# Stationary weight blocks 64 bytes further on, and products before a norm that end tile by tile

## What is computed

```
# first block, two layers i; (h: 256 tokens, hc: 256 context tokens)
h = h + 0.5 * m2 * (silu(a) * b) @ ffn_w_out[i, 0]      # a, b = split(modnorm(h) @ ffn_w_in[i, 0])
y = fourier(modnorm(h)) @ fnet_w_out                    # i = 0
y = (silu(g) * norm(retention(q, k, v))) @ ret_w_out    # i = 1; q, k, v, g = modnorm(h) @ ret_w_in
h = h + m5 * y
h = h + 0.5 * m8 * (silu(a) * b) @ ffn_w_out[i, 1]
...
# second block, two layers l
f = (silu(n @ ff1_w_gate) * (n @ ff1_w_up)) @ ff1_w_down     # n = rmsnorm(h, pre)
h = h + 0.5 * rmsnorm(f, post)
m = concat(ssd, pool, attention)(rmsnorm(h) @ w_in) @ w_out
h = h + rmsnorm(m, mix_post)
f = (silu(n @ ff2_w_gate) * (n @ ff2_w_up)) @ ff2_w_down
h = h + 0.5 * rmsnorm(f, post)
```

## Time and profile before

| | us |
|---|---|
| median of 3 runs | 2917.98 |
| lowest and highest | 2908.57, 2922.2 |
| profiled execution | 2915.53 |
| its span, first to last instruction | 2913.7 |
| TensorE busy in it | 2789.5 |
| VectorE busy | 1703.9 |
| ScalarE busy | 1153.1 |
| mean granted TensorE clock | 0.987 of full speed |

### The profile page before, as it was taken

One profiled execution on the slowest core, in us unless ns is written; L12 is line 12 of the kernel. 1 busy time (PEld: TensorE's weight loads), 2 busy tenths in 40 slices (PEclk: granted clock), 3 DMA queues, 4 the chain that ended last, 5 costly groups with the idle time before them and its releaser, 6 DMA issues.

```text
span 2913.7 us, 43918 instructions
## 1 busy us (share of the span) xinstructions
PE 2789.5 (96%) x18214; PEld 2496.8 (86%) x18214; DVE 1703.9 (58%) x2029; ACT 1153.1 (40%) x1442; POOL 0.9 (0%) x13
## 2 busy tenths in 40 slices
PE   6999999999999999999999999999989999998998
PEld 3878878778887888878998999999779999997897
DVE  3774654677325753443356655655766566576764
ACT  4322224422224223243254544444545444454443
POOL 0000000000000000000000000000000000000000
PEclk8999999999999999999999999999999999999999
DMA  6654531456233663634223565664326656642463
GB/s 234 195 177 132 172 121 37 130 181 187 92 98 102 202 188 106 195 101 125 88 87 123 173 187 166 178 212 130 119 75 200 192 156 194 188 124 68 149 184 120
DMA packets 371094, 428.69 MB, mean 147 GB/s; under 512 B 13952, under 2 KB 351104, under 8 KB 370816
## 3 DMA queue, kind: packets, MB, share of 16 engines
q1 hardware_dynamic: 370224, 424.79, 47.6%
q10 hardware_dynamic: 720, 1.74, 0.2%
HBM read 425.43 MB, written 1.05 MB: 146 GB/s over the span
## 4 chain that ended last, share of the span: by engine, by line
PE 85%; DVE 8%; ACT 4%; issue 2%; DMA 1%; SPq 0%; DVEq 0%; ACTq 0%
PE ps L949 25%; PE ps L950 25%; PE ps L951 25%; PE ps L967 3%; ACT w_hi L678 1%; DVE w_lo L687 1%; PE ps L1106 1%; DVE rstd L1096 1%; DMA raw<-in_w_mod 1%; PE ps L1275 1%; DVE tmp L1201 1%; PE ps L773 1%; DVE cx L1778 1%; DVE h L1206 1%; PE ps L1653 0%
## 5 line engine op out<-in xcount | busy, mean ns | idle before, releaser
L687 DVE TENSOR_TENSOR w_lo<-raw,w_hi 128x1024 fp32r<-128x1024 f32 (+1 forms) x672 | 800.0, 1199 | 898.5 <-ACT w_hi L678 891.9
L949 PE MATMUL ps<-u_hi,w_hi 128*128 128x256 f32 (+1 forms) x3520 | 1123.1, 319 | 37.8 <-DVE w_lo L687 8.9
L951 PE MATMUL ps<-u_hi,w_lo 128*128 128x256 f32 (+1 forms) x3520 | 1114.3, 317 | 0.0
L950 PE MATMUL ps<-u_lo,w_hi 128*128 128x256 f32 (+1 forms) x3520 | 1114.3, 317 | 0.0
L678 ACT ACTIVATE w_hi<-raw 128x1024 fp32r<-128x1024 f32 (+1 forms) x672 | 690.8, 1035 | 1032.7 <-PE ps L951 947.2
L949 PEld LDWEIGHTS ps<-u_hi,w_hi 128*128 128x128 f32 x3520 | 664.3, 189 | 100.5 <-issue 29.1
L951 PEld LDWEIGHTS ps<-u_hi,w_lo 128*128 128x128 f32 x3520 | 666.1, 189 | 46.8
L950 PEld LDWEIGHTS ps<-u_lo,w_hi 128*128 128x128 f32 x3520 | 665.7, 189 | 45.7
L949 PE MATMUL ps<-g_hi,w_hi 128*128 128x256 f32 (+1 forms) x1408 | 450.8, 320 | 0.0
L951 PE MATMUL ps<-g_hi,w_lo 128*128 128x256 f32 (+1 forms) x1408 | 450.1, 320 | 0.0
L950 PE MATMUL ps<-g_lo,w_hi 128*128 128x256 f32 (+1 forms) x1408 | 450.1, 320 | 0.0
(11 more groups left out here) (234 smaller groups left out, 2036.7 us busy)
## 6 DMA issues: line engine op xcount, KB each, us to landing
raw<-in_ffn_w_in SPq DMA_DIRECT2D x176, 512.0 KB, 4.3
raw<-in_w_mod SPq DMA_DIRECT2D x144, 512.0 KB, 4.4
raw<-in_ff_w_gate SPq DMA_DIRECT2D x88, 512.0 KB, 4.3
raw<-in_ff_w_up SPq DMA_DIRECT2D x88, 512.0 KB, 4.3
raw<-in_ffn_w_out SPq DMA_DIRECT2D x64, 512.0 KB, 3.4
raw<-in_ff_w_down SPq DMA_DIRECT2D x64, 512.0 KB, 3.5
raw<-in_ret_w_in SPq DMA_DIRECT2D x48, 512.0 KB, 3.5
raw<-in_w_in SPq DMA_DIRECT2D x36, 512.0 KB, 3.8
```

Source lines behind the costliest of these rows:

```text
L687: dve.tensor_tensor(w_lo[:, slot, at], raw[:, raw_slot, 0:cols], w_hi[:, slot, at].bitcast(f32), ALU.subtract).then_inc(lo_ready, 1)
L949: pe.matmul(out, w_hi[:, slot, cols], hi, start=first, stop=False, **check)
L950: pe.matmul(out, w_hi[:, slot, cols], lo, start=False, stop=False, **check)
L951: return pe.matmul(out, w_lo[:, slot, cols], hi, start=False, stop=last, **check)
```

## The change

Two things. `WEIGHT_SHIFT` = 16 floats moves the stationary blocks in `w_hi` and `w_lo` by 64 bytes, from 128 to 192 modulo 256, for ScalarE and VectorE that write them and for TensorE that reads them; products in `mode="tokens"` keep their places. And in the 12 products above the last two units of the last pair go tile by tile. `pe_tail` does tile 6 in both units, then tile 7; between the two units of tile 7 it sums `acc`. ScalarE (`act_tail`) squares each tile by itself, in a `store` product straight from PSUM; VectorE (`dve_tail`) copies or adds each tile by itself, and adds up the squares of the pairs before at fixed turns.

More of the change, by code:

```diff
@@ L31 @@
 SHIFT, ROOM = 48, 64
+WEIGHT_SHIFT = 16
 EPS = 1e-6
@@ L105, in counts @@
         if self.squares:
-            out["sq"], out["sum"] = 4, 2
+            out["sq"], out["sum"], out["tail"] = 5, 2, 1
+            out["resid_tail"] = int(evac_adds(self))
         if self.norm_after:
@@ L182, in hold_last_splits @@
             s.holds_last = after is not None and after.kind == "stats" and any(x.kind == "gemm" for x in stages[j + 1:])
-        elif s.kind == "stats" and gemm is not None and gemm.holds_last:
+        elif s.kind == "stats" and gemm is not None and gemm.squares:
+            s.more["begun"] = True
+            if not gemm.holds_last:
+                gemm = None
+                continue
             s.more["held"] = next(x for x in stages[j + 1:] if isinstance(x, Gemm))
@@ L688, in split_lo, with stream @@
                               ALU.subtract).then_inc(lo_ready, 1)
-        def stream(eng, g, t, nxt, split, evacuate, norm, beside=None):
+        def stream(eng, g, t, nxt, split, evacuate, norm, tail, beside=None, added_squares=None):
             t_next = {"unit": t["unit"] + g.n * g.units}
@@ L921, in dve_evacuate @@
                 for b in range(2):
[L922 to L926, removed]
+                    ins = dve_add_residual(dve, g, it * 4 + 2 * pair + b, ps[:, 2 * pair + b, :])
                 ins.then_inc(done, 1)
@@ L1001, in turn @@
                 for u, (pair, k0, kt) in enumerate(g.order(it)):
+                    if g.squares and u == g.units - 2 and it_is_second(it):
+                        pe_tail(pe, g, t, it)
+                        return
                     if g.k_major and it_is_first(it):
@@ L1096, in dve_stats, with pe_stat_sums @@
             dve.reciprocal(rstd[:, 0:n], rstd[:, 0:n]).then_inc(rstd_ready, 1)
+        def pe_stat_sums(pe, n, sums):
+            pe.wait_ge(sums_ready, sums)
+            for i in range(2):
+                pe.matmul(ps[:, STAT, 0:n], ones[:, :], acc[:, i, 0:n], start=i == 0, stop=False)
         def pe_stats(pe, g, t):
@@ L1100, in pe_stats @@
             sums, squares = (t["sum"] + 2, t["sq"] + 4) if more else (t["sum"], t["sq"])
-            pe.wait_ge(sums_ready, sums)
+            if not g.more.get("begun"):
+                pe_stat_sums(pe, n, sums)
             for i in range(2):
-                pe.matmul(ps[:, STAT, 0:n], ones[:, :], acc[:, i, 0:n], start=i == 0, stop=False)
-            pe.wait_ge(squares_ready, squares)
-            for i in range(2):
+                if g.more.get("begun"):
+                    pe.wait_ge(squares_ready, squares - 1 + i)
+                elif i == 0:
+                    pe.wait_ge(squares_ready, squares)
                 ins = pe.matmul(ps[:, STAT, 0:n], ones[:, :], tmp1[:, i, 0:n], start=False, stop=i == 1)
@@ L1946, in _ @@
                         act_load_root(act)
-                    stream(act, g, t, follower(whole, j), split_hi, act_evacuate, act_stats)
+                    stream(act, g, t, follower(whole, j), split_hi, act_evacuate, act_stats, act_tail)
                 elif g.kind == "squares":
```

32 lines of the change are left out of this document (27 added, 5 removed).

## The result

The changed kernel is slower: 2965.53 us, the median of four runs (2961.85 to 2969.47), against 2920.09 for the kernel before, measured again beside it (2908.57 to 2930.26). The ratio is 1.0176, with an interval of 1.0141 to 1.021. The profiled execution took 2969.47 us (span 2967.7), against 2915.53 (2913.7) before: +53.9 us. The forecast was 2876 us in a range of 2848 to 2932, so the time lies above the range. Of the rivals the third, slower at 2952 us, came nearest.

A forecast was written before the change was run, and what follows sets the result against it. TensorE was taken as the bound, busy for 96% of the span and 85% of the chain. -17 - 12 - 2.5 - 11 = -42.5 us from 2915.5 gave 2873, plus 2.5 for the median: 2876 us, range 2848 to 2932.

The forecast's parts named there:

- the third: Rival: distance 128 is the worst, 256-column matmuls go to 121.5 ns, +34 us in all, 2952 us; chance 0.18.
- part one (a): 9456 matmuls with 256 columns, distance 64 to 128 bytes: all take 113.4 ns, -17 us.
- part one (b): 5136 matmuls with 512 columns, distance 0 to 64 bytes: 2.3 ns less each, -12 us, between 0 and -34.
- two states: 256-column matmuls at distance 64: a stretch keeps 113.4 ns (lower) or 117.7 ns (upper) between pauses of TensorE.
- the 264-column unit: Unit whose last-block matmuls at distance 128, corrected for eight columns, gave the upper bound of 121.5 ns for 256 columns.
- Part one (c): 576 matmuls with `both` or packed, distance 0 to 64 bytes: from 120.0 to 113.4 or 117.7 ns, -2.5 us.
- Part two: Tile-by-tile tails of the 12 products that a norm follows: shorter way to the root, -11 us, between 6 and 14 saved.
- The first rival: Distance 64 frees the 512-column matmuls wholly, 220 ns, -34 us in place of -12, 2854 us; chance 0.20.
- The second: Rival: addresses count for no more than the draw of the state; only the tail's -11 us is left, 2907 us; chance 0.24.

The follow-up runs named there:

- the last version: Changed kernel with weights at 192 modulo 256 bytes only in the pieces with `both`, 128 elsewhere, tails kept: 2908.52 us against 2921.3 for the kernel before, ratio 0.9954.

## Why the prediction was wrong

**The bound was right.** TensorE is the chain, and a nanosecond per matmul counted in full. Busy time and chain share say so, and so does the sum that closes on 54 us. That the distance is what counts, as the prediction read from three values, is right too: the weights moved alone cost 1.9%, and the same place with the distance kept cost nothing.

Of the 96.5 us between the forecast's -42.5 and the +54 measured, part one (a) makes 52 and part one (b) 45. Both steps failed.

**Part one (b), the 512 columns, is the step that failed by its bounds.** The prediction put the step from distance 0 to 64 between -6.6 ns and nothing, took -2.3 and got -12 us. It measured +6.5 ns, +33 us. The error was to carry the step over from 256 columns, where it is in fact -2 to -7 ns (`both` gained 4.2 in the mean), and then to set the upper bound at "nothing at all", with no row that excluded a loss. That 226.7 is twice 113.4 was noted as a sign that 512 columns may be free of the conflict already, and that reading held in so far as no distance gave less.

**Part one (a), the 256 columns, was taken at the wrong end.** The bounds, 113.4 and 121.5, did hold: 118.9. The prediction took the lower end because two states at distance 64 and one value at distance 0 looked like one conflict that fades with distance. Distances 96, 128 and 192 show that it doesn't fade; 64 is the exception. Nor are two states a mark of the good distance: at 128 there are two as well, 118.7 and 120.0, both above those of 64. The nearest row of the very distance, the 264-column unit, spoke for the upper end, was 2.6 ns too high by the correction for eight columns, and was set aside. In place of -17 us it was +35.

**Part one (c)** was right: -2.5 us forecast, -2.4 measured, with the two states appearing in the pieces with `both` as soon as these stand at 64. The size hangs on which states came up: in the trace with the weights alone moved it is 114.7 ns, -3.0 us.

**Part two** was right: -11 us forecast, -12 as summed from the two profiled executions, and the tails alone gave 0.4%. By kind, from the last matmul's start to the root: 512 tokens 3.14 forecast and 3.19 measured, with 1.7 in the stream; the `store` products 1.56 and 1.49 (2.42 and 2.36 with the sum in the stream); the residual with 256 tokens 2.04 and 2.04. In the first `mix_out` the wait in the stream was 0.19 us in place of 0.4. Nothing queued behind the new waits came late: the waits of the 256-column group on `u_hi` add up to 22.9 us after and 23.1 before.

**The rule on the ports.** The weights alone, moved by 64 bytes, made TensorE's matmuls 3% slower at the full clock, 226.8 to 233.3 ns, with no instruction added. The Trainium skill (TensorE: Matmul & The Clock Gate, "Step-by-step: what each phase is for") has the weight load and the moving operand read through ports of their own, so that loading takes nothing from the running matmul. The prediction read from it, as a rival, that no start address would matter, and that reading falls: the spacing of these fp32r matmuls, back to back, does depend on where the two operands stand to one another. Whether it is a load that takes something from a running matmul, no run here shows, so the page's sentence itself is neither borne out nor refuted.

**The rivals.** The third had the right sign, and it decides from 118 ns on, where the measurement is 118.9. That its 2952 us lies so near is partly luck: it priced (a) at +60 us, 25 too high, and (b) at -12, 45 too low. At 118.9 and with the forecast's (b) it gives 35 - 12 - 2.5 - 11 = +9.5 us, and only with (b) at +33 does it come to +54. The first rival needed 220 ns with 512 columns, which no distance gave. The second, that addresses count for no more than the draw, is the one that the counts rule out. Its draw is real, though: between all stretches low and all high lie 9456 x 4.4 = 41 us, and the executions of one program on one chip spread by up to 28 us (the tails alone, 2886.52 to 2914.21). The one of these that was traced is the longest, and it is mostly in the upper state; that the others differ from it by their states is likely but not traced.

## What to carry to other kernels

Where TensorE is the bound and its matmuls run back to back, read the spacing from start to start by shape and by stretch, and note for each the distance between stationary and moving operand modulo 256 bytes: it is worth 3% with 512 columns and 6% with 256, and the best distance of one shape is not that of another. Don't carry a step in address from one shape over to another, and where a shape already stands at its best known spacing, bound an edit of its addresses with a loss. Look at the states before comparing two traces: in one pair here they hid a gain of 12 us. A change of two parts should be measured as two: here a tail worth 12 us was buried under a shift that cost 66.

## What the runs showed of the hardware

With fp32r operands and 128x128 stationary blocks, at a granted clock of 1.00 (the 2.4 GHz level), the spacing of back-to-back matmuls depended on the distance of the operands modulo 256 bytes, in steps as fine as 16 bytes: 512 columns took 226.8 ns at 0, 229.8 at 16, 233.3 at 32 and 64, 232.5 at 128, 228.9 at 192, 233.3 at 224 and 227.1 at 240; 256 columns took 120.0 at 0, 118.3 at 32, 118.1 at 48, 119.0 at 80, 118.3 at 96, 118.9 at 128 and 117.5 at 192. These are means over one execution each.

At distance 64 the 256 columns have two spacings, 113.3 and 117.8 ns. Every stretch of over 1000 matmuls keeps one of them from one pause of TensorE to the next, and which one it is changes between stretches and between kernels: the stretch at 1870 us was in the upper one in the kernel before, with the tails alone and in the last version, and in the lower one with everything moved 64 bytes on. With 512 columns at distance 16 the same thing shows, 226.7 in some stretches and 233.3 in others, and with 256 columns at distance 128, 118.7 and 120.0. What decides it was not tried, and since each kernel was traced once, no run shows whether it changes between executions of one program.

A `w_lo` block out of place slows the matmuls with `w_hi` too, and the reverse, so that the spacing isn't a property of one matmul and its two operands alone. Whether the weight loads, the reads of the moving operand or something between them is what meets, no run here can tell.
